# Weighted values of a pair of heads in one run, and score waits by half

## The reference, cut to what matters

```
for each block of 128 query rows:
    lc = q @ kc.T * scale + bias        # compressed keys (63 of them)
    ls = q @ k_slc.T * scale + bias     # selected blocks of keys; all of them here (16 of 16)
    lw = q @ k_win.T * scale + bias     # a window of 512 keys
    lf = fq @ fk.T * scale + cq - ck    # the second mixer ("FoX"), causal
    o_nsa = g0 * softmax(lc) @ vc + g1 * softmax(ls) @ v_slc + g2 * softmax(lw) @ v_win
    o_fox = softmax(lf) @ fv
```

## Time and profile before

| | us |
|---|---|
| median of 3 runs | 2399.66 (2397.24 to 2399.71) |
| the profiled execution's own time | 2398.11 |
| its span, first to last instruction | 2396.3 |
| prompt attention, within the span | about 338 to 713 |
| mean granted clock of TensorE | 0.998 |

### The profile page before, as it was taken

How to read it: one execution, slowest core, us unless ns; L and a number is a source line. 1 busy time by engine, 2 the same in 40 slices (tenths; PEclk the granted TensorE clock), 3 DMA queues, 4 the chain that set the end, 5 groups by cost and what they waited for, 6 DMA issues and landing times.

```text
span 2396.3 us, 30680 instructions
## 1 busy us (share of the span) xinstructions
PE 2345.8 (98%) x10983; PEld 1531.9 (64%) x10983; DVE 1217.1 (51%) x3023; ACT 541.9 (23%) x1300; POOL 830.4 (35%) x874
## 2 busy tenths in 40 slices
PE   8999999999999999999999999999999999999999
PEld 4544665666666776788885468888888874443343
DVE  4886727676763444424224774333343324329765
ACT  0001016666663333111111221111111100001132
POOL 0000005555543001666653434343343337203531
PEclk9999999999999999999999999999999999999999
DMA  5423820021039786432225101111111126434101
GB/s 187 107 75 85 288 98 37 1 94 49 2 117 262 233 229 186 173 85 80 80 90 151 66 23 54 41 49 36 45 45 36 36 78 204 158 135 151 71 18 57
DMA packets 185952, 240.25 MB, mean 100 GB/s; under 512 B 53435, under 2 KB 128833, under 8 KB 184265
## 3 DMA queue, kind: packets, MB, share of 16 engines
q1 hardware_dynamic: 181018, 218.99, 29.7%
q0 software_dynamic: 3616, 9.73, 1.2%
q10 hardware_dynamic: 1168, 9.58, 1.2%
HBM read 216.18 MB, written 37.99 MB: 106 GB/s over the span
## 4 chain that ended last, share of the span: by engine, by line
PE 56%; DVE 2%; ACT 1%; issue 0%; DVEq 0%; ACTq 0%
PE ps L2249 36%; PE ps L2413 11%; PE ps L2302 5%; PE ps L2470 2%; PE ps L2400 1%; DVE xT L152 1%; PE ps L2478 1%; ACT xT L2523 0%; PE ps L2306 0%; DVE arena L3001 0%; ACT arena L2620 0%; DVE stats L2675 0%; PE ps L2345 0%; DVE queries L3004 0%; DVE arena L1397 0%
## 5 line engine op out<-in xcount | busy, mean ns | idle before, releaser
L2249 PE MATMUL ps<-xT,arena 128*128 128x272 f32 x1920 | 472.7, 393 | 1.3 <-DVE arena L1406 1.3
L2249 PEld LDWEIGHTS ps<-xT,arena 128*128 128x128 f32 x1920 | 363.9, 190 | 76.9 <-DVE arena L1406 1.7
L2249 PE MATMUL ps<-queries,arena 128*128 128x272 f32 x1312 | 332.5, 393 | 1.8 <-DVE queries L2816 1.0
L2249 PEld LDWEIGHTS ps<-queries,arena 128*128 128x128 f32 x1312 | 249.7, 190 | 53.9 <-DVE queries L2816 1.4
L235 PE MATMUL ps<-arena,xT 128*128 128x512 f32 (+1 forms) x512 | 198.9, 551 | 1.2 <-issue 0.8
L235 PEld LDWEIGHTS ps<-arena,xT 128*128 128x128 f32 x512 | 98.0, 192 | 101.6 <-issue 94.2
L2249 PE MATMUL ps<-arena 128*128 128x272 f32 x576 | 148.5, 394 | 0.0
L974 ACT ACTIVATE arena<-arena 128x640 f32<-128x640 f32 (+10 forms) x208 | 136.9, 660 | 39.1 <-DVE arena L924 33.3
L2413 PE MATMUL ps<-arena 128*128 128x512 f32 x312 | 140.6, 599 | 0.0
L1039 POOL TENSOR_SCALAR arena<-arena,gates 128x640 f32<-128x640 f32 (+15 forms) x156 | 101.7, 664 | 93.4 <-DVE arena L938 93.4
L816 PE MATMUL ps<-arena,queries 64*128 64x512 f32 (+10 forms) x704 | 118.5, 451 | 14.0 <-DVE arena L924 9.4
(11 more groups left out here) (357 smaller groups left out, 3375.0 us busy)
## 6 DMA issues: line engine op xcount, KB each, us to landing
arena<-in_cache_fox_kv SPq DMA_DIRECT2D x72, 256.0 KB, 4.0
arena<-in_w_ffn_down SPq DMA_DIRECT2D x68, 256.0 KB, 3.5
arena<-in_w_in SPq DMA_DIRECT2D x16, 1024.0 KB, 5.3
xT<-in_w_ffn_down SPq DMA_DIRECT2D x64, 256.0 KB, 3.7
xT<-in_cache_fox_kv SPq DMA_DIRECT2D x56, 256.0 KB, 6.0
arena<-in_cache_nsa_kv SPq DMA_DIRECT2D x64, 192.0 KB, 7.7
arena<-in_w_ffn_up SPq DMA_DIRECT2D x11, 1024.0 KB, 5.4
arena<-in_w_ffn_gate SPq DMA_DIRECT2D x11, 1024.0 KB
```

Of the source, the lines that this page charges most:

```text
L2249: mm = pe.matmul(ps[:, first + BANK_OF[z], 0:PIECE], weight[:, j, :], moving[:, j, :], start=(j == 0 and z in (1, 6, 5, 7)), stop=(j == kk ...
```

## The change

The values of an odd pair q are all issued in round q + 1: both parts, one behind the other. The round q + 2 has none, and the last call of values_beside goes. In scores(p), the wait for the logits is split: ahead of the first matmul of half 0 it asks only for half 0 of the pair waited for, ahead of the first of half 1 for half 1 too.

```
         def _(pe):
             def scores(p):
                 wait_for = p.n if p.wide or (p.n and PAIRS[p.n - 1].wide) else p.n - 1
-                if wait_for > 0:
-                    pe.wait_ge(logits_done, PARTS_BEFORE[wait_for])
                 pieces = [(b, first + s, s, w) for b, first, width in p.parts for s, w in split(width)]
                 for b, at_, s, w in pieces:
                     for half in range(2):
+                        if at_ == 0 and wait_for > 0:
+                            pe.wait_ge(logits_done, parts_until(wait_for - 1, half))
                         rows = slice(half * HD, (half + 1) * HD)
...
             def values_beside(n):
-                for part in (1, 0):
-                    q = n - 1 - part
-                    if 0 <= q < NPAIR and PAIRS[q].j == 1:
-                        weighted_values(PAIRS[q], part)
+                if 0 <= n - 1 < NPAIR and PAIRS[n - 1].j == 1:
+                    for part in range(2):
+                        weighted_values(PAIRS[n - 1], part)
...
             values_beside(NPAIR)
-            values_beside(NPAIR + 1)
```

## The result

| | kernel before | changed kernel |
|---|---|---|
| median (lowest to highest of 5) | 2399.66 us (2395.39 to 2400.09) | 2412.02 us (2408.92 to 2415.44) |
| ratio, 95% interval | | 1.0055, 1.0041 to 1.0070 |
| profiled execution | 2398.1 us | 2408.9 us |
| its span | 2396.3 us | 2407.1 us |

The change makes the kernel slower by 0.4 to 0.7%, 12.4 us by the medians and 10.8 by the profiled executions. The forecast was 2408.5 us, with 60 chances in 100 on 2404.5 to 2413.

What follows compares the result with a forecast made beforehand. TensorE's own work bounds the prompt's attention (busy 357 of 375 us). Terms 6.4 + 6.5 - 1.8 - 1.6 = +9.5 us, about 0.5 absorbed, gave 2407 profiled, 2408.5 as median; range 2404.5 to 2413, 60 in 100.

Steps and rivals of the forecast that it cites:

- loop: Attention: wide score runs wait for the previous pair's logits, a cycle of 3.64 us whatever TensorE does in between.
- free: Five shortened gaps per turn that nothing else holds; each merged value run there saves its fixed 0.16 us.
- Term 1: Attention gaps shortened by the move but held by VectorE's logits give back little: +6.4 us, ends +2 and +10.
- Term 2: Shortened gaps where transposes wait for GpSimd, in even two-chunk pairs behind a late copy and inverse: +6.5 us.
- the far end of the range: Upper end, +8 us, for GpSimd-held gaps, if ScalarE's output copies behind an exponential delay a value run too.
- Term 3: Half waits in score runs give earlier logits but free no array time: -1.8 us, ends -12.6 and 0.
- the first half can start 0.88 earlier, its logits too: Pair 13's score run: the early half brings earlier logits, the next run's 0.98 us wait goes, its gap shrinks 0.62.
- Term 4: Merged value runs each save a fixed 0.16 us, counted only in free short gaps: -1.6 us, ends 0 and -7.
- The absorption: Behind the attention, TensorE's wait for a cache page takes up about 0.5 us of the stage's loss.
- The heavier pile-up: Rival: logits-held gaps cost 10 us, GpSimd-held ones 8, only 1 comes back: +17, 2413 to 2417 us; 15 in 100.
- That of lost overlap: Rival: a wait between score-run halves makes them run one after the other, 2420 us and above; 5 in 100.

Runs made afterwards that it cites:

- values_only: Kernel before with only the new order of value runs, the score wait still ahead of both halves: 2416.25 us, ratio 1.0075.
- after_inv: Changed kernel with VectorE's inverse issued ahead of its copy of a pair's second part: 2411.95 us, ratio 1.0062.
- half_mixed: Kernel before with half waits, first-half matmuls first in score runs 13 and 25, values merged for pairs 3, 15, 27 of a turn: 2392.41 us, ratio 0.9977.

## Why the prediction was right, and where it wasn't

A place is the gap that got longer and the one that got shorter (T(9) and T(21) with the gap in which they wait).

| place | forecast | measured |
|---|---|---|
| loop: gaps 37-38, 41-42, 43-44, 45-46 (each twice) | 0.39, 0.27, 0.68, 0.85 | 0.53, 0.28, 0.82, 0.86 |
| loop: 47-48, 49-50, 51-52 | 0.51, 0.52, 0.99 | 0.85, 0.68, 1.01 |
| T(9), T(21) (twice) | 0.83, 1.17 | 0.79, 1.19 |
| T(33), T(28), T(16) (twice) | 0.26, 0.27, 0.05 | 0.37, 0.47, 0.25 |
| T(4), T(52), end | 0.48, 0.48, 0.41 | 0.68, 0.68, 0.58 |
| half waits: tile 5 (twice), gaps 25-28 (twice), opening | -0.52, -0.16, -0.39 | -0.40, +0.06, -0.40 |
| free: 8, 20, 32, 36, 40 (twice) | -0.16 each | -0.14, -0.15, -0.15, -0.16, +0.21 |
| terms 1 to 4 | 6.4, 6.5, -1.8, -1.6 | 7.5, 8.1, -1.1, -0.8 |
| stage | +9.5 | +13.7 |

**The mechanism was right.** Odd gaps grew by the full value time, short gaps gave back only what neither logits, GpSimd nor ScalarE held, and values_only gave the same costs without the half waits. Reading value time minus slack at each gap, from one trace, came within 0.02 us at T(21), gaps 41-42, 45-46 and 51-52.

**Term 1 was 1.1 us too small.** Two sizes were off. The second part of a window pair's values costs more than its records: the last four are on 39 rows instead of 128, and the starts around that change stand 0.31 and 0.26 us apart instead of 0.21. That is 0.15 a run, in 37-38, 43-44 and 49-50. And for gap 48 I took 0.34 us off because its logits wait for a bias load. In the changed kernel that load was issued 13.5 us ahead of S(48) instead of 11.9, and the logits still start 2.26 us behind it, as before. The late start isn't the load; what it is I leave open.

**Term 2 was 1.6 too small, and its cause half wrong.** GpSimd holds T(9), T(21), T(33) and T(38) (2.4 us net). I had missed T(38), where gap 40 was counted as free. But the even pairs of two parts don't wait for an inverse behind a copy: after_inv moved nothing, and ScalarE's copy lets T(4) go 0.2 us later than GpSimd would. The output bank, which I costed at nothing because I saw nobody on TensorE wait for it, and kept as the far end of the range, holds V(8) and V(20), with GpSimd close behind at T(9) and T(21): taking GpSimd away gave 0.5 at each, taking the bank's copy too gave 2.2 us in the stage. That was misread: in the kernel before three value runs do wait for that copy, two for 0.08 us each and the last of the stage for 0.61:

```profile
709.65 2.40 PE L848 MATMUL ps<-xT,arena 128*64 128x128 f32 x40 [0.61 <-ACT queries L989]
```

**Term 3 was 0.7 too large.** The step that failed is "the first half can start 0.88 earlier, its logits too". The first half started at once, but its logits began 1.24 us behind the previous ones instead of 0.77. In the changed kernel, by the modelled ends of the single records, the first half's last matmul is through the array at 396.39, the second half's first, ahead of it in the program, at 396.81, and VectorE starts at 396.87:

```profile
394.81 2.43 PE L816 MATMUL ps<-arena,queries 64*128 64x512 f32 x8 [0.68 <-DVE arena L922]
...
396.87 0.96 DVE L922 CUSTOM_DVE_ANT_0 xT<-ps,arena 128x768 f32<-128x768 f32 x1 [0.75 <-PE ps L816]
```

In half_mixed the first half's last is at 395.50 and VectorE starts at 395.54. A matmul's signal came only after those ahead of it in the program, also where they ran in the other half of the array. The Trainium skill says this in "TensorE: Matmul & The Clock Gate", Part 3, The mechanism: matmuls start and end strictly in program order. These runs agree, and I had drawn only on the same part's rule that they run concurrently. That one held too: an early half freed no array time (V(44) comes 4.92 us after S(46) with it and without).

**Term 4** was right in size, 0.14 to 0.16 for each merged run in a free gap, and wrong for gap 40, which GpSimd holds.

**The absorption** was 2.9 us, not 0.5: 0.4 by which the stage began early, 1.4 at the wait for the page and just behind it, 0.3 at a wait for VectorE 230 us further on, and 0.7, net, by a half-speed clock period that the kernel before had and this one hadn't. The stage came 4.2 us longer than forecast and the rest gave back 2.4 more, of which 0.4 and 0.7 are accidents of the two traces, so the nearness of the total is partly luck. The heavier pile-up, +17, was the closest rival. That of lost overlap fell: S(46) takes 1.35 us as before.

**Two signs were badly chosen.** I had said that the stage's idle time would rise by some 8 us; it fell to 16.0, since a half-started run counts as busy. And I had said that term 1 is wrong if S(47) follows S(46) in under 3.6 us. From start to start it is 2.95, because the first half starts early; the loop still takes its 3.64 us, which only the second half and V(44) show.

## What to carry to other kernels

Where one engine is nearly full and others feed it, filler work is worth what it covers: before moving it, take for each stretch that gets shorter its length less the slack, for every engine that feeds its end, since a second holder stood close behind the first: 0.2 us at T(4), and at V(8) the 0.43 us that a free output bank gave were 0.13 in the end, because GpSimd held T(9) again. Splitting a wait by half pays in full only if that half's own work stands together in the program, so that its signal can come early. And a change of two parts should be run apart: here one was a gain of 0.14% inside a loss.

## What the runs showed of the hardware that I hadn't expected

On few columns GpSimd's scaling costs mostly its start: 0.45 us on 128 columns, 0.39 on 64, 0.37 on 7, against 1.0 on 896. The half-speed clock came at S(25)'s wait of 1.88 us in values_only and cost 1.69 us. It didn't come at the same wait in that kernel's second turn, 1.88 us too, nor at the shorter ones of the kernel before (1.29) and of the changed kernel (0.73); no run here tells why. And a trace of this stage repeats to 0.01 us in each gap, while whole executions of one kernel differ by 4 to 7 us.
